# Queries of the first weight block split by token tile in the key-score stage of a two-block transformer kernel

## The chip, the cores and the metric

One core of a Trainium2 chip runs the whole program in one launch. The metric is the device time of that core in microseconds (us), median of several runs. Engines are named as in the profile: PE (TensorE matmul), PEld (its weight load), DVE (VectorE), ACT (ScalarE), POOL (GpSimd), SP (the queue that loads weights).

## The reference

Two layers of a latent/context block with a product-key expert layer, then two layers of a hybrid mixer with memory attention; 256 tokens, width 1024, fp32. The part that matters here is how the expert layer picks its experts:

```
def block(xc):                       # 128 tokens
    q = (xc @ wq).reshape(C, 8, 2, 128)                # 16 "half heads" of 128
    s = einsum('chpd,hpnd->chpn', q, sub_keys)         # 128 scores for each half head
    s1, i1 = top_k(s[:, :, 0], 16);  s2, i2 = top_k(s[:, :, 1], 16)
    cand = s1[..., :, None] + s2[..., None, :]         # 256 sums for each head
    top, pos = top_k(cand, 16);  eidx = cidx[pos]
    g = softmax(top)
    a = gelu(einsum('chkd,cd->chk', u_tab[eidx], xc))
    return einsum('chk,chkd->cd', g * a, v_tab[eidx])
```

The modulation vectors of both layers (silu(c) @ ada_w, six times 1024 values for each layer) are also needed; the kernel spreads that product over other stages.

## The kernel before, in words

The program is a row of stages. Each is a block in which every engine has its own list of instructions, and a barrier closes it. A stage is written once and can run in three settings: alone; beside the modulation sums (`run_with_sums`, L437); or as a guest inside an expert stage, beside the gathers (`run_guest`). The test `hosted()` is true in the last setting only.

**The key-score stage** (`keys_stage`, L1799) runs for token pair s of layer l. The tokens are two tiles of 128. PE turns the 16 sub-key matrices (L1819) and DVE copies them to SBUF (L1854). Then comes a list of items. An item is one half head h for one tile or for both. PE computes the query of the item: 8 matmuls of 128 x 128 weights with 256 columns (both tiles) or 128 (one tile), L1830; the trace shows two records for each. ACT copies it (L1891), PE multiplies it with the keys (`dot`, L1847; one matmul a tile), and ACT copies the scores to `sims` (L1896). PE issues the dot of item i after the product of item i+1, and the product of item i needs ACT's copy of item i-3. The weights of wq come in four blocks of four half heads. Before the change only block 3 is split by tile: 12 whole items, then 4 for tile 0 and 4 for tile 1, 20 in all (0 to 19).

**The search** runs on DVE in the same stage, for tile 0 of the pair only. For every quarter q (two heads, half heads 4q to 4q+3) there are three pieces: the top 16 of half heads 4q and 4q+1 (L1931 to L1935), the same of 4q+2 and 4q+3, then the candidates (L1953) and their top 16, followed by `pair_indices` (L1991 to L2014) for the quarters 0 to 2, and after quarter 0 the writing of the first picks (L2018, L2022). The first piece needs the scores of half head 4q+1, the others those of 4q+3. In the program's order a piece stands behind the step of item i as soon as the item that it needs is i-2 or lower. What is left of the picks of quarter 3 is done in the next stage, `last_picks` (L2024).

**The modulation sums** (`ModulationSums`) are a list of rows, 8 to a block, each 512 columns wide. For a block that both streams need, DVE makes one stream's step of a row (L846 for the first row of a block, L849 for the others), after which ACT scales the row for the other (L866), and POOL adds it (L884; the first row of a block needs no add). For a block of one stream only ACT and POOL work. The weights of four rows come in one DMA of 1 MB that POOL issues (L897) into one of two slots, when POOL has added the rows that were in the slot; at row 4n of its list it asks for the load of rows 4n+4 to 4n+7. When a block is added, PE sums it over the partitions (L911).

Where the rows stand among the other work is fixed by a pace when the program is written. Each item of the key stage is worth 5.0 us (both tiles), 2.15 us (tile 0) or 0 us (tile 1); DVE gets one row for every 2.0 us in layer 0 (`sums.host(keys, 2.0, ...)`, L2524) and for every 3.4 us in layer 1 (L2554), in both cases before the search pieces of that item. ACT does the rows that belong to item i before it copies the query of item i. Rows that are left go to `last_picks`: there ACT and POOL do them first. Layer 0 has rows up to 112, of which DVE has work in those below 96; the stage begins at row 77. Layer 1 has 48, the stage begins at row 32, and DVE has no work in any.

**What POOL does behind the rows**: in the key stage it issues the first 4 (layer 0) or 6 (layer 1) expert gathers; in `last_picks` it issues gathers up to row 6 (9), waits for all sums and issues three more. `last_picks` ends on DVE with an addition of the summed modulation (L966 in layer 0, L972 in layer 1), which waits for PE's last L911. The expert stage then starts with DVE's L2205 and its 512 gathered rows (L2226 and others).

The key stage runs outside an expert stage twice (layer 0 and layer 1, token pair 0), and once as a guest. In layer 1 it also ends with turned memory tiles: PE transposes four pairs into the PSUM banks 0 to 3 (`turn_memory`, L1809) and ACT takes them out with `gain_memory_pair`.

Of the kernel before, what the change touches and what calls it, by code (L numbers as in the profile page):

```python
# [127 lines left out]
def build_kernel(nc, io, out):  # L128
# [61 lines left out]
    def open_stage():  # L190
        for s in every:
            s.base = s.total
# [200 lines left out]
    def hosted():  # L393

        return host[0] and host[0].block
# [255 lines left out]
    def column(name, j):  # L651
        return columns[:, where[name][0] + j:where[name][0] + j + 1]
# [1146 lines left out]
    def keys_stage(l, s):  # L1799


        open_stage()
        split = (3,)
        items = [(4 * b + j, t, n) for b in range(4) for t, n in (((0, 1), (1, 1)) if b in split else ((0, 2),)) for j in range(4)]
        last = len(items) - 1
        keys_t = lifted[:, 2048 * s:2048 * s + 2048]
        qt = [proj[:, 2 * P * i:2 * P * (i + 1)] for i in range(4)]

        def turn_memory(pe):  # L1809
            for g in range(4):  # L1810
                if g == 3:
                    pe.wait_ge(*read_a.at(dots_at(last - 1)))
                turn_memory_pair(pe, g, g)

        def tensor(pe):
            w = take(pe, ("keys", l))
            for g in range(4):
                for q in range(4):
                    mm = pe.transpose(psum[:, g, q * P:q * P + P], w[:, 4 * g + q, :], ident)  # L1819
                mm.then_inc(*products.one())  # L1820
            release()
            for i, (h, t0, nt) in enumerate(items):
                if h % 4 == 0 and t0 == 0:
                    w = take(pe, ("wq", l, h // 4))
                yield 4 + asked_at(i)
                pe.wait_ge(*(emptied if hosted() else read_v).at(4))
                if i >= 3:
                    pe.wait_ge(*read_a.at(asked_at(i - 3)))
                for k in range(KD):
                    mm = pe.matmul(psum[:, i % 3, 0:P * nt], w[:, k, (h % 4) * P:(h % 4) * P + P],  # L1830
                                   turned_s[s][:, k, P * t0:P * (t0 + nt)], start=k == 0, stop=k == KD - 1)
                mm.then_inc(*products.one())
                if h % 4 == 3 and t0 + nt == 2:
                    release()
                if i >= 1:
                    dot(pe, i - 1)
            dot(pe, last)
            if l == 1:
                turn_memory(pe)
# [33 lines left out]
        def asked_at(i):  # L1873
            return 2 * i if i else 1

        def dots_at(i):
            return 2 * i + 3 if i < last else 2 * last + 2

        def scalar(act):
            for g in range(4 if hosted() else 0):  # L1880
                yield g + 1
                act.wait_ge(*products.at(g + 1))
                act.copy(keys_t[:, 512 * g:512 * g + 512], psum[:, g, :]).then_inc(*emptied.one())
            for i in range(last + 2):
                if i <= last:
                    w = P * items[i][2]
                    yield 4 + asked_at(i)
                    act.wait_ge(*products.at(4 + asked_at(i)))
                    if i >= 4:
                        act.wait_ge(*products.at(4 + dots_at(i - 4)))  # L1890
                    act.copy(qt[i % 4][:, 0:w], psum[:, i % 3, 0:w]).then_inc(*read_a.one())  # L1891
                if i >= 1:
                    h, t0, nt = items[i - 1]
                    yield 4 + dots_at(i - 1)
                    act.wait_ge(*products.at(4 + dots_at(i - 1)))
                    act.copy(sims[:, t0:t0 + nt, h, :], psum[:, 3 + (i - 1) % 3, 0:P * nt].rearrange("p (t n) -> p t n", t=nt))\  # L1896
                       .then_inc(*read_a.one())
            if l == 1:
                for g in range(4):
                    gain_memory_pair(act, 0, g, g)  # L1900

        run_stage(tensor, vector, scalar)
        if l == 0:
            lifted_free[s] = products.now()
# [590 lines left out]
    def to_keys(l, s):  # L2495

        tiles = [2 * s, 2 * s + 1]
        return [lambda: turn_mixed(s, HALVED),
                lambda: linear_stage([([("w_out", l, b)], "rows", tiles, normed, ("add", lambda t: gate_row(0, s), 512 * b))
                                      for b in range(2)], ahead=memory_root() if l == 1 else None),  # L2500
                lambda: norm_stage(tiles, lambda k, t: first_gain(1, k, s), lambda k, t: first_shift(1, k, s)),
                lambda: turn_back(s), lambda: keys_stage(l, s)]
# [115 lines left out]
    def turn_memory_pair(pe, g, bank):  # L2618
        for i in range(2):
            k = 2 * g + i  # L2620
            for t in range(2):
                mm = pe.transpose(psum[:, bank, 256 * i + P * t:256 * i + P * t + P], mixed_v[:, 2 + t, k * P:k * P + P], ident)
        mm.then_inc(*filled.one())

    def gain_memory_pair(act, l, g, bank):
        act.wait_ge(*filled.at(g + 1))
        for i in range(2):
            k = 2 * g + i
            ins = act.activation(turned_s[1][:, k, :], psum[:, bank, 256 * i:256 * i + 256], ACT.Copy,
                                 scale=column("norm_mem_w_2", 8 * l + k))  # L2630
        ins.then_inc(*emptied.one())
# [586 lines left out]
```

## Time and profile before

| | us |
| --- | --- |
| median of 3 runs | 3812.22 |
| runs | 3797.35 to 3813.24 |
| profiled execution, its own time | 3829.47 |
| its span | 3827.7 |
| PE busy | 2777.0 (73%) |
| DVE busy | 2517.3 (66%) |
| POOL busy | 1683.3 (44%) |
| ACT busy | 793.1 (21%) |
| layer 0, key stage and the picks after it | 363 to 453 |
| layer 1, the same | 2246 to 2326 |

A busy share is a mean over stages with different limits. What the change is worth is read from the two stretches of the last lines, 170 us of the span.

### The profile page before, as it was taken

The numbers are of one execution on the slowest core, as the hardware profiler recorded it, in microseconds if no ns is written. First come the engines' busy times: TensorE is split into PE (matmuls) and PEld (weight loads), VectorE is DVE, ScalarE is ACT, GpSimd is POOL, SyncE is SP. The second block draws the span as 40 slices with busy tenths as digits, with TensorE's granted clock in tenths as the row PEclk, the third lists the DMA queues.
The fourth block names the chain that finished last, engine by engine and source line by source line (L and its number), as shares of the span: only waits on it lengthen the run. The fifth ranks groups of instructions, "written<-read, shape, count | busy, mean of one in ns | idle before, by whom it ended". The sixth has DMA issues, their size and how long they took to land. (4 is left out here: it accounts for less than half of the span.)

```text
span 3827.7 us, 31086 instructions
## 1 busy us (share of the span) xinstructions
PE 2777.0 (73%) x8573; PEld 1444.4 (38%) x8573; DVE 2517.3 (66%) x5611; ACT 793.1 (21%) x2031; POOL 1683.3 (44%) x1722
## 2 busy tenths in 40 slices
PE   7998675777787676863086886358516799899998
PEld 3455632213462232221022565133202265566555
DVE  3665978777786678878855457887786536533542
ACT  2243200222122200210022431012002213410331
POOL 2333565674546555665665244667666600000000
PEclk9998888996899888986599897679758999999999
DMA  7534699998999899998999448999999954234321
GB/s 268 181 126 165 242 384 393 347 362 288 365 353 362 320 400 404 366 357 303 373 356 334 156 177 312 374 380 389 385 404 362 360 206 149 77 144 143 128 88 72
DMA packets 353335, 1086.55 MB, mean 284 GB/s; under 512 B 32657, under 2 KB 41357, under 8 KB 352013
## 3 DMA queue, kind: packets, MB, share of 16 engines
q0 software_dynamic: 232592, 849.45, 58.8%
q1 hardware_dynamic: 120572, 235.12, 17.4%
q8 instruction: 72, 1.18, 0.1%
q14 instruction: 99, 0.80, 0.1%
HBM read 1080.21 MB, written 4.24 MB: 283 GB/s over the span
## 5 line engine op out<-in xcount | busy, mean ns | idle before, releaser
L2260 ACT ACTIVATE heads<-common,dots 128x128 f32<-128x128 f32 x768 | 279.9, 396 | 778.0 <-PE psum L2276 362.4
L1269 PE MATMUL psum<-ring,turned 128*128 128x512 f32 (+1 forms) x800 | 344.4, 589 | 49.9 <-issue 32.1
L2226 DVE SCALAR_TENSOR_TENSOR lent<-lent,psum 128x1024 f32<-128x1024 f32 x274 | 323.2, 1218 | 48.6 <-ACTq L482 24.6
L2276 PE MATMUL psum<-lent,heads 128*128 128x512 f32 x524 | 289.0, 652 | 73.2 <-DMA lent<-in_peer_v_dram,picks_u 36.3
L2276 PE MATMUL psum<-proj,heads 128*128 128x512 f32 x374 | 207.3, 655 | 178.2 <-issue 160.2
L2316 POOL DMA_INDIRECT lent<-in_peer_u_dram,picks_u x274 | 257.4, 939 | 176.9 <-DVE lent L2226 90.3
L2316 POOL DMA_INDIRECT lent<-in_peer_v_dram,picks_u x262 | 251.4, 960 | 129.8 <-issue 61.0
L1721 PE MATMUL psum<-ring,turned 128*128 128x512 f32 x512 | 234.7, 617 | 38.4 <-issue 14.7
L2234 DVE SCALAR_TENSOR_TENSOR psum<-lent,dots,psum 128x512 f32<-128x512 f32 x262 | 197.8, 755 | 96.9 <-DMA lent<-in_peer_v_dram,picks_u 60.2
L2226 DVE SCALAR_TENSOR_TENSOR proj<-proj,psum 128x1024 f32<-128x1024 f32 x195 | 232.2, 1218 | 28.0 <-issue 14.4
L1269 PEld LDWEIGHTS psum<-ring,turned 128*128 128x128 f32 x800 | 161.0, 203 | 228.7 <-issue 216.9
L2276 PE MATMUL psum<-turned,heads 128*128 128x512 f32 x258 | 149.3, 681 | 132.2 <-issue 110.6
L2316 POOL DMA_INDIRECT proj<-in_peer_u_dram,picks_u x195 | 183.6, 941 | 117.4 <-DVE proj L2226 60.6
L2316 POOL DMA_INDIRECT proj<-in_peer_v_dram,picks_u x187 | 179.2, 958 | 101.5 <-issue 46.8
L2276 PEld LDWEIGHTS psum<-lent,heads 128*128 128x128 f32 x524 | 87.2, 195 | 271.1 <-DMA lent<-in_peer_v_dram,picks_u 181.3
L2234 DVE SCALAR_TENSOR_TENSOR psum<-proj,dots,psum 128x512 f32<-128x512 f32 x186 | 140.4, 755 | 70.1 <-DMA proj<-in_peer_v_dram,picks_u 43.0
L884 POOL TENSOR_TENSOR gate_rows<-heads,gate_rows 128x512 f32<-128x512 f32 x80 | 107.5, 1344 | 177.9 <-ACT heads L866 162.4
L2276 PEld LDWEIGHTS psum<-proj,heads 128*128 128x128 f32 x374 | 65.3, 199 | 310.9 <-issue 226.1
L2316 POOL DMA_INDIRECT turned<-in_peer_u_dram,picks_u x135 | 127.2, 942 | 125.3 <-DVE turned L2226 50.7
L2276 PE MATMUL psum<-heads 128*128 128x512 f32 x130 | 75.1, 661 | 137.8 <-ACT heads L2260 96.0
L2226 DVE SCALAR_TENSOR_TENSOR turned<-turned,psum 128x1024 f32<-128x1024 f32 x135 | 161.2, 1218 | 18.0 <-issue 8.7
L1721 PEld LDWEIGHTS psum<-ring,turned 128*128 128x128 f32 x512 | 100.2, 198 | 169.3 <-issue 141.8
(388 smaller groups left out, 5430.6 us busy)
## 6 DMA issues: line engine op xcount, KB each, us to landing
ring<-in_w_in_dram SPq DMA_DIRECT2D x37, 2048.0 KB
proj<-in_ada_w_dram POOLq DMA_DIRECT2D x20, 1024.0 KB, 5.7
heads<-in_ada_w_dram POOLq DMA_DIRECT2D x20, 1024.0 KB, 6.0
ring<-in_peer_wq_dram SPq DMA_DIRECT2D x10, 2048.0 KB
lent<-in_w_in_dram SPq DMA_DIRECT2D x9, 2048.0 KB, 7.8
ring<-in_w_out_dram SPq DMA_DIRECT2D x9, 2048.0 KB
lent<-in_w_out_dram SPq DMA_DIRECT2D x5, 2048.0 KB, 8.1
ring<-in_w_mk_dram SPq DMA_DIRECT2D x4, 2048.0 KB
```

What stands on the lines that cost most here:

```text
L884: pool.tensor_tensor(out=acc, in0=self.weights(self.row_pool), in1=acc, op=ALU.add)\
L1269: mm = pe.matmul(psum[:, b % nb, 0:cols], lhs(k, it), w[:, kk, :], start=k == 0, stop=k == k_total - 1)
L1721: mm = pe.matmul(psum[:, 2 * ((q + i) % deep), :], turned_s[place][:, k, i * P:i * P + P], w[:, k, :], start=k == 0, stop=k == KD - 1)
L2226: dve.scalar_tensor_tensor(out=src, in0=src, scalar=1.0, in1=kept_row, op0=ALU.mult, op1=ALU.mult, accum_out=weight).then_inc(rows_used.se ...
L2234: dve.scalar_tensor_tensor(out=acc, in0=part, scalar=weight, in1=acc, op0=ALU.mult, op1=ALU.add)\
L2260: act.activation(diags[n % DIAGS], ident, ACT.Copy, scale=dots[:, j:j + 1]).then_inc(diag_ready.sem, 1)
L2276: pe.matmul(kept_row[:, 0:512], diags[n % DIAGS], row_slot(r)[:, 0:512], start=j == 0, stop=j == PICKS - 1).then_inc(pe_rows.sem, 1)
L2316: pool.indirect_dma_start(out=row_slot(r), out_offset=None, in_=tables_dram[which], in_offset=bass.IndirectOffsetOnAxis(ap=picks_u[:, t, j ...
```

## The change

Where the stage is not a guest of an expert stage, block 0 of wq is split like block 3. The items are then 24 (0 to 23): the four half heads of block 0 for tile 0, the same four for tile 1, 4 whole items each for blocks 1 and 2, and block 3 as before. Item 0 to 3 are worth 2.15 us each to the pace and items 4 to 7 nothing. Layer 1's fourth memory pair goes to the bank that the last dot but one has left, now bank 4 and no longer bank 3.

```diff
         open_stage()
-        split = (3,)
+        split = (3,) if hosted() else (0, 3)
         items = [(4 * b + j, t, n) for b in range(4) for t, n in (((0, 1), (1, 1)) if b in split else ((0, 2),)) for j in range(4)]
         last = len(items) - 1
+        free_bank = 3 + (last - 1) % 3
...
                 if g == 3:
                     pe.wait_ge(*read_a.at(dots_at(last - 1)))
-                turn_memory_pair(pe, g, g)
+                turn_memory_pair(pe, g, g if g < 3 else free_bank)
...
                 for g in range(4):
-                    gain_memory_pair(act, 0, g, g)
+                    gain_memory_pair(act, 0, g, g if g < 3 else free_bank)
```

## Rows read from the trace of the kernel before

**Rows 1.** Waits of the layer 0 stretch (363 to 453): total us, times, longest.

```profile
DVE gate_rows L849 <- DMA heads<-in_ada_w_dram: 6.9, 1, 6.9
```

**Rows 2.** Timeline, start of layer 0's stage: start, us, engine, line, [idle before].

```profile
363.15 3.39 DVE L849 SCALAR_TENSOR_TENSOR gate_rows<-heads,silu_c,gate_rows 128x512 f32<-128x512 f32 x3
367.99 2.33 DVE L849 SCALAR_TENSOR_TENSOR gate_rows<-proj,silu_c,gate_rows 128x512 f32<-128x512 f32 x3
368.75 0.37 ACT L1891 COPY proj<-psum 128x256 f32<-128x256 f32 x1 [3.31 <-PE psum L1830]
371.74 0.77 POOL L897 DMA_DIRECT2D heads<-in_ada_w_dram  x1 [0.30 <-POOL gate_rows L884]
377.23 2.33 DVE L849 SCALAR_TENSOR_TENSOR gate_rows<-heads,silu_c,gate_rows 128x512 f32<-128x512 f32 x3 [6.91 <-DMA heads<-in_ada_w_dram]
379.47 0.48 DVE L1931 MAX8 heads<-proj 128x8 f32<-128x128 f32 x2
387.24 0.48 DVE L1931 MAX8 heads<-proj 128x8 f32<-128x128 f32 x2
```

**Rows 3.** Timeline of PE, layer 0: whole and half products, a step apart.

```profile
413.54 3.62 PE L1830 MATMUL psum<-turned,ring 128*128 128x256 f32 x16
417.44 3.62 PE L1830 MATMUL psum<-turned,ring 128*128 128x256 f32 x16
426.47 1.95 PE L1830 MATMUL psum<-turned,ring 128*128 128x128 f32 x16
428.48 1.95 PE L1830 MATMUL psum<-turned,ring 128*128 128x128 f32 x16
```

**Rows 4.** Timeline of DVE, layer 0: quarters 1 and 2.

```profile
398.33 5.08 DVE L849 SCALAR_TENSOR_TENSOR gate_rows<-heads,silu_c,gate_rows 128x512 f32<-128x512 f32 x4
407.10 0.49 DVE L1931 MAX8 heads<-proj 128x8 f32<-128x128 f32 x2 [1.35 <-ACT proj L1896]
412.45 0.20 DVE L1991 CAST heads<-heads 128x64 f32<-128x64 uint32 x1
419.39 3.53 DVE L2011 TENSOR_TENSOR lifted<-lifted,heads 128x512 f32<-128x512 f32 x2
431.70 0.41 DVE L1991 CAST heads<-heads 128x64 f32<-128x64 uint32 x1
434.81 1.32 DVE L2011 TENSOR_TENSOR lifted<-lifted,heads 128x512 f32<-128x512 f32 x2
```

**Rows 5.** Timeline of POOL, PE and DVE, layer 0: adds, and the picks stage.

```profile
412.77 5.55 POOL L884 TENSOR_TENSOR gate_rows<-heads,gate_rows 128x512 f32<-128x512 f32 x4 [0.47 <-ACT heads L866]
445.46 0.20 DVE L1991 CAST heads<-heads 128x64 f32<-128x64 uint32 x1 [0.60 <-PEq L438]
446.24 1.29 POOL L884 TENSOR_TENSOR gate_rows<-heads,gate_rows 128x512 f32<-128x512 f32 x1 [9.88 <-ACTq L438]
447.68 1.84 PE L911 MATMUL psum<-common,gate_rows 128*128 128x1 f32 x8 [8.36 <-POOL gate_rows L884]
452.27 0.39 DVE L966 TENSOR_TENSOR soft<-psum,columns 128x32 f32<-128x32 f32 x2
453.03 0.93 POOL L2316 DMA_INDIRECT heads<-in_peer_u_dram,picks_u  x1 [0.30 <-POOLq L438]
453.23 1.23 DVE L2205 COPY psum<-mixed 128x1024 f32<-128x1024 f32 x1 [0.57 <-PEq L438]
```

**Rows 6.** Timeline, layer 1's stage.

```profile
2248.74 7.15 PE L1830 MATMUL psum<-turned,lent 128*128 128x256 f32 x32 [1.36 <-DVE lifted L1854]
2260.67 0.49 DVE L1931 MAX8 heads<-proj 128x8 f32<-128x128 f32 x2 [12.08 <-ACT proj L1896]
2268.47 0.49 DVE L1931 MAX8 heads<-proj 128x8 f32<-128x128 f32 x2 [5.36 <-ACT proj L1896]
2283.67 0.37 ACT L1896 COPY proj<-psum 128x256 f32<-128x256 f32 x1
2285.81 0.46 DVE L1931 MAX8 heads<-proj 128x8 f32<-128x128 f32 x2
```

## The prediction

> **What bounds the kernel now.** PE and DVE are the busiest engines over the span, but the change touches only two stretches of it, so I read the waits of those stretches first and then their timelines engine by engine. The reader is to see that the search on DVE sets the end of both key stages, and what makes it late.
>
> In layer 0 it is not the scores. DVE idles 6.9 us for the weights of a sum row [rows 1] and only 1.35 us for scores [rows 4]. Ten rows stand ahead of the first search piece (items 0 to 3, 20 us at one row for 2.0 us). DVE is through seven by 370.3, waits until 377.23 for the load that POOL issued at 371.74 (5.5 us), and searches from 379.47 [rows 2]. After that it has no wait but the 1.35 us at 407.10 [rows 4].
>
> In layer 1 DVE has no row work and does wait for scores: 12.08 us, then 5.36 us; from 2268.47 on it has work to the end of the stage [rows 6].
>
> **PE's share.** A whole item takes 3.90 us from start to start (413.54 to 417.44), a half one 2.01 us (426.47 to 428.48), both with their dots [rows 3]. Block 0 costs 8 x 2.01 = 16.1 instead of 4 x 3.90 = 15.6 us: 0.5 us more for every later item; between nothing and 1 us. Four more copies of each kind on ACT hide between products: ACT waited 3.31 us for the first one [rows 2].
>
> **Order in layer 0, changed.** The pace now gives 4 rows (77 to 80) for items 0 to 3, none for 4 to 7, then 2, 3, 2, 3, 2, 3 for items 8 to 13, 2 and 3 for 14 and 15, and one each for 16 to 19: the stage ends at 77 + 57.2/2 = row 105. Before it was 77 + 68.6/2 = 111. So six rows, 105 to 110, move behind the stage.
>
> *Quarter 0.* DVE is through row 80 at 368.0. Item 0 is delayed by the slow clock at the start: its copy came at 368.75 where 3.6 us of product from 363.4 give 367.0, so 1.7 us. Half items then end near 367.0 and 368.8, the dot of item 1 after item 2 at 371.0, its copy at 371.6: the search starts there, 7.9 us sooner. The first piece took 2.3 us, so 374.0; item 3's scores are copied at 375.6 (two items later), and the rest of quarter 0 with the first picks takes 398.33 - 387.24 = 11.1 us [rows 2, 4]: 386.7, where before it was 398.3. So far 11.6 us are gained, but before DVE had rows 77 to 91 done there, and now has 77 to 80.
>
> *The rows that are late.* Rows 81 to 83 take 0.78 us each beside a quiet POOL [rows 2], to 389.0; 84 to 87 at 1.13 to 393.5. POOL has added row 83 at 392.6 (ACT's scaling, then 1.39 us a row [rows 5]), so only now asks for rows 88 to 91: 392.9 + 5.5 = 398.4. DVE stands idle 4.9 us. Before, that load was hidden behind the search. Rows 88 to 90 to 401.8; the first piece of quarter 1 from there, against 403.4 (398.33 + 5.08) [rows 4]; then rows 91 to 95, five of 1.1 us, which before were done: 401.8 + 2.4 + 5.6 = 409.8, where the second piece began at 407.10. **The stage is 2.7 us later** from there on. Quarters 1 to 3 have the same work. Bounds: 0 (if the five rows find POOL quiet and the load lands in 3 us) to 6 (if the load of rows 92 to 95 is waited for as well).
>
> *A contended port.* In quarter 1, L2011's two instructions took 3.53 us with POOL adding beside them; in quarter 2, 1.32 us [rows 4]. From its first instruction to the end of L2011 the index work took 412.45 to 422.92 in quarter 1, 10.5 us, and 431.70 to 436.13 in quarter 2, 4.4 us: 6 us of blocking. In the changed order POOL's adds for rows 97 to 103 fall at about 415 to 427, on quarter 1's index work again, so I add nothing here; 0 to 3 us either way. The Trainium skill (SBUF — State Buffer, on port contention) says that DVE and GpSimd share a port pair, that one instruction holds it to its end and the other blocks. By that rule six adds moved beside the last index work would stretch it too; this trace agrees with 3.53 against 1.32 us.
>
> *Picks stage.* Before, one add (row 111) was left to it: POOL 446.24 to 447.53, PE's L911 to 449.5, and DVE's index work hid both, reaching L966 at 452.27, 6.8 us after its start [rows 5]. Now seven adds are left (105 to 111): 0.8 + 7 x 1.42 = 10.7 us after the start, PE 2.0, DVE's wake-up 0.1, so L966 at 12.8. **That is 6.0 us more.** The index work, 6.8 us before and stretched by up to those 6 us, stays just under it. POOL's gathers of rows 4 to 8 begin 8.7 us later relative to the stage; before, the last began 0.2 us ahead of the barrier, and the first four gathers are in already; DVE uses row 4 some 6 us after the barrier, so I take no stall. If the barrier waits for their issue it is 1.5 to 3 us more. Bounds 5 to 9 us.
>
> Layer 0: 2.7 + 6.0 = 8.7 us later.
>
> **Layer 1.** Rows need no DVE, so the search starts with the scores. From 2248.74: item 1 to 2252.3, item 2 with dot 0, dot 1, copy: 2255.1 instead of 2260.67. The second piece at 2259.1 instead of 2268.47, that is 9.4 us sooner [rows 6]; quarter 0 ends at 2274.1 instead of 2283.5. But item 9 (half head 5) has its scores only at 2276.7, and item 11 (half head 7) 0.5 us after their old 2284.0 (copy of 2283.67 + 0.37): 2284.5. Before, DVE came for them at 2285.81 [rows 6], only 1.8 us behind. **Of 9.4 us, 1.3 are left.** Then the adds: before, all 16 rows were issued by item 10 and POOL turned to gathers before quarter 1; now they run to item 18, beside the index work of quarters 1 and 2. What quarter 0 loses to adds lies inside the slack that DVE now has; three adds beside quarter 1 cost up to 2 us, of which I take 0.8. All 48 rows are done in the stage (57.2/3.4 = 16.8), so the picks stage keeps its size. I take -1.3 + 0.8 = -0.5 us, bounds -3 to +4.
>
> The bank change orders nothing new: the same last dot but one is waited for. It is nothing, or half a microsecond for the later PE end, under the search by 1.8 us.
>
> **Sum.** +8.7 - 0.5 = +8.2 us. The profiled execution, 3829.5, would be 3837.7. It stands 17.3 us (0.45%) over the median of the runs shown; with the same difference on 3812.2 I forecast 3820.4.
>
> **Rivals.**
>
> 1. *The head start is kept* (faster). For: DVE has 8.3 us of idle in layer 0 and 17.4 in layer 1 ahead of the search. If the load of rows 88 to 91 came in time and POOL took its seven adds under the index work, layer 0 would win 8.3 - 3.6 - 1.6 = 3; in layer 1 up to 9.4 if quarter 1 did not catch up with PE. Some 12 us: 3800. Against: PE has no gap in which to bring item 11 forward. Chance 0.17.
> 2. *The late sums cost more* (slower than the forecast, and clearly slower than before). One mechanism: rows displaced behind the search make POOL late. It decides from the point at which the barrier after the picks holds until POOL has issued its five gathers: start + 10.9 + 5 x 1.25 + 0.5 = 17.7 instead of 7.8, so +9.9 and not +6; with 2.7, and 4 in layer 1 from adds beside two index runs, 17 us: 3829. For: gathers are issued by the same engine in order. Against: the last one started only 0.2 us before DVE's next work. Chance 0.18.
> 3. *Nothing is seen*: later work makes up what the start loses, because the expert stage waits on gathers, not on DVE's start; 3812. Against: POOL itself starts its gathers 11 us later in layer 0. Chance 0.15.
>
> The forecast itself: 0.50; its own range 3813 to 3828.
>
> **From these to the numbers.** About 0.5% (19 us) is what a measurement of this kernel can tell from no change. Every case above is inside it except part of rival 2 (17 us with an uncertainty of some 6) and what the 16 us between the runs shown add on either side. Faster 0.11, same 0.73, slower 0.16. The range 3798 to 3837 takes in rivals 1 to 3.
>
> **What would show it.** In layer 0: first L1931 near 371.6; L846 and L849 of rows 88 to 90 only after quarter 0, with an idle on a DMA of ada_w of about 5 us ahead of them; seven L884 after the last block line and L966 waiting for PE; L2205 near 462. In layer 1: first L1931 near 2255 relative to the old 2260.7, a wait of 2 to 3 us ahead of quarter 1 and one of 5 ahead of its second piece, the stage's end within 2 us of its old length. Wrong would be: no DMA wait in layer 0 (then it is nearer rival 1), L966 not waiting for PE's L911, or quarter 1 of layer 1 starting its second piece more than 3 us sooner.

## The result, and the profile after

The changed kernel takes 3825.36 us (median of 8 runs), the kernel before 3809.29 us (8 runs). The ratio is 1.0038, 95% interval 1.0023 to 1.0054: 14.5 us slower (8.8 to 20.6), inside the 0.5% that the prediction called "same", yet the interval leaves out zero. The two medians lie 16.1 us apart. The forecast was +8.2 us.

One profiled execution of each can't show this: the changed kernel's (3824.36 us) is 5.1 us shorter than that of before, since the work outside the two stretches differs from run to run by more than the change is worth: from the end of the first stretch to the start of the second it took 1792.9 us before, 1772.4 us after, and 1789.5 us in e1, whose layer 0 code is the same as that of the changed kernel. What repeats is the length of the two stretches. From here on **the layer 0 stretch** runs from DVE's first sum row in the key stage to the start of the expert stage (L2205, now L2206), and **the layer 1 stretch** from the first key copy to the same point. Layer 0: 453.23 - 363.15 = 90.08 us before, 472.09 - 368.13 = 103.96 after. Layer 1: 79.52 and 78.95. Together +13.3 us.

The timeline of DVE in layer 0, changed kernel (start, us, engine, line, [idle before it]), answers to [rows 2, 4]:

```profile
368.13 3.39 DVE L849 SCALAR_TENSOR_TENSOR gate_rows<-heads,silu_c,gate_rows 128x512 f32<-128x512 f32 x3
...
376.48 0.49 DVE L1932 MAX8 heads<-proj 128x8 f32<-128x128 f32 x2 [4.56 <-ACT proj L1897]
...
380.50 0.49 DVE L1932 MAX8 heads<-proj 128x8 f32<-128x128 f32 x2 [1.58 <-ACT proj L1897]
...
391.61 3.41 DVE L849 SCALAR_TENSOR_TENSOR gate_rows<-proj,silu_c,gate_rows 128x512 f32<-128x512 f32 x3
395.12 7.30 DVE L849 SCALAR_TENSOR_TENSOR gate_rows<-heads,silu_c,gate_rows 128x512 f32<-128x512 f32 x4
403.73 1.51 DVE L846 TENSOR_SCALAR gate_rows<-proj,silu_c 128x512 f32<-128x512 f32 x1 [1.30 <-DMA proj<-in_ada_w_dram]
...
406.74 0.48 DVE L1932 MAX8 heads<-proj 128x8 f32<-128x128 f32 x2
...
415.40 5.09 DVE L849 SCALAR_TENSOR_TENSOR gate_rows<-heads,silu_c,gate_rows 128x512 f32<-128x512 f32 x4 [5.31 <-DMA heads<-in_ada_w_dram]
420.40 0.48 DVE L1932 MAX8 heads<-proj 128x8 f32<-128x128 f32 x2
...
431.76 3.43 DVE L2012 TENSOR_TENSOR lifted<-lifted,heads 128x512 f32<-128x512 f32 x2
...
446.89 1.29 DVE L2012 TENSOR_TENSOR lifted<-lifted,heads 128x512 f32<-128x512 f32 x2
```

Take 368.13 off and compare with 363.15 taken off before: the search starts at +8.35 instead of +16.32, quarter 0 ends at +23.5 instead of +35.2, and then the gain is gone. The second piece of quarter 1 starts at +52.3 instead of +44.0, although its first piece is 1.6 us sooner (+38.6 instead of +40.2). Rows 91 to 95 now stand between the two pieces, and four of them waited 5.31 us for weights that before lay there.

POOL, PE and DVE at the end of the stretch, changed kernel, answering to [rows 5]:

```profile
457.52 0.19 DVE L1992 CAST heads<-heads 128x64 f32<-128x64 uint32 x1 [0.60 <-PEq L438]
458.30 4.13 POOL L884 TENSOR_TENSOR gate_rows<-proj,gate_rows 128x512 f32<-128x512 f32 x3 [15.81 <-ACT proj L866]
462.57 6.53 POOL L884 TENSOR_TENSOR gate_rows<-heads,gate_rows 128x512 f32<-128x512 f32 x4
464.56 3.41 DVE L2012 TENSOR_TENSOR lifted<-lifted,heads 128x512 f32<-128x512 f32 x2
469.25 1.84 PE L911 MATMUL psum<-common,gate_rows 128*128 128x1 f32 x8 [9.74 <-POOL gate_rows L884]
471.12 0.39 DVE L966 TENSOR_TENSOR soft<-psum,columns 128x32 f32<-128x32 f32 x2 [1.42 <-PE psum L911]
472.09 1.23 DVE L2206 COPY psum<-mixed 128x1024 f32<-128x1024 f32 x1 [0.57 <-PEq L438]
474.31 0.94 POOL L2317 DMA_INDIRECT heads<-in_peer_u_dram,picks_u  x1 [0.30 <-issue]
```

Seven adds stand where one stood, L966 waits for them, and the stage takes 14.6 us instead of 7.8. The last line shows that the barrier does not wait for POOL's gathers: the fifth starts 2.2 us after DVE has begun the expert stage. (The kernel opens these blocks with `no_gpsimd_drain=True`; no run does without it.)

Layer 1, DVE, changed kernel, answering to [rows 6]:

```profile
2253.48 0.49 DVE L1932 MAX8 heads<-proj 128x8 f32<-128x128 f32 x2 [6.52 <-ACT proj L1897]
2257.51 0.49 DVE L1932 MAX8 heads<-proj 128x8 f32<-128x128 f32 x2 [1.58 <-ACT proj L1897]
2275.12 0.49 DVE L1932 MAX8 heads<-proj 128x8 f32<-128x128 f32 x2 [4.19 <-ACT proj L1897]
2282.92 0.49 DVE L1932 MAX8 heads<-proj 128x8 f32<-128x128 f32 x2 [5.36 <-ACT proj L1897]
...
2323.43 1.23 DVE L2206 COPY psum<-mixed 128x1024 f32<-128x1024 f32 x1 [0.58 <-PEq L438]
```

DVE starts 5.6 us sooner relative to the stage. It then stands 4.19 us ahead of quarter 1's first piece and 5.36 us ahead of its second, 9.6 us where before it waited for no scores.

### The profile page after: what moved, and what is told of

It reads as the page before. It is cut to its first block and busy times, and to the rows that moved or that the text cites. A ratio compares the mean times of both kernels' runs of the same rounds, so it can differ in the third digit from the quotient of the medians.

```text
span 3822.6 us, 31382 instructions
## 1 busy us (share of the span) xinstructions
PE 2789.8 (73%) x8701; PEld 1455.1 (38%) x8701; DVE 2524.9 (66%) x5611; ACT 793.3 (21%) x2047; POOL 1683.6 (44%) x1722
## 5 line engine op out<-in xcount | busy, mean ns | idle before, releaser
L1269 PE MATMUL psum<-ring,turned 128*128 128x512 f32 (+1 forms) x800 | 335.3, 577 | 46.2 <-issue 31.9
L1721 PE MATMUL psum<-ring,turned 128*128 128x512 f32 x512 | 240.7, 630 | 37.1 <-issue 17.6
L1269 PEld LDWEIGHTS psum<-ring,turned 128*128 128x128 f32 x800 | 156.8, 198 | 220.4 <-issue 211.9
L884 POOL TENSOR_TENSOR gate_rows<-proj,gate_rows 128x512 f32<-128x512 f32 x60 | 79.6, 1327 | 211.2 <-ACT proj L866 207.3
```

The costliest lines, as they stand in the source:

```text
L884: pool.tensor_tensor(out=acc, in0=self.weights(self.row_pool), in1=acc, op=ALU.add)\
L1269: mm = pe.matmul(psum[:, b % nb, 0:cols], lhs(k, it), w[:, kk, :], start=k == 0, stop=k == k_total - 1)
L1721: mm = pe.matmul(psum[:, 2 * ((q + i) % deep), :], turned_s[place][:, k, i * P:i * P + P], w[:, k, :], start=k == 0, stop=k == KD - 1)
```

## The experiments

The stretches are read from one profiled execution each. "Index work" is the time at which the first index instruction of a quarter starts, from the start of the stretch; the fourth is the start of the picks stage. Ratios are to the kernel before, timed together with the run; "profiled once" stands where a run has no such timing.

| run | first piece | index work 0, 1, 2 | picks stage | layer 0 | layer 1 | ratio (95%) |
| --- | --- | --- | --- | --- | --- | --- |
| before | 16.3 | 29.4, 49.3, 68.6 | 82.3 | 90.1 | 79.5 | 1 |
| changed | 8.4 | 17.7, 57.6, 75.8 | 89.4 | 104.0 | 79.0 | 1.0038 (1.0023 to 1.0054) |
| e1 layer 0 only | 8.2 | 17.6, 57.4, 75.7 | 89.2 | 103.8 | 79.4 | 1.0034 (1.0017 to 1.0052) |
| e2 layer 1 only | 14.6 | 27.8, 47.7, 66.7 | 80.5 | 88.3 | 79.0 | 1.0009 (0.9988 to 1.0030) |
| e3 pace of before for items 0 to 3 | 15.1 | 22.8, 59.0, 78.0 | 94.2 | 101.9 | 78.2 | 1.0027 (1.0011 to 1.0043) |
| e4 pace 1.6 | 6.6 | 16.0, 54.6, 73.6 | 91.2 | 98.1 | 79.0 | profiled once |
| e5 DVE order of before | 15.9 | 29.5, 59.2, 77.4 | 91.0 | 98.8 | 79.0 | 1.0018 (1.0004 to 1.0033) |
| e6 2 MB load left out | 8.2 | 17.6, 53.9, 72.1 | 85.7 | 100.2 | 79.0 | profiled once |
| e7 rows fed by item | 9.1 | 17.8, 49.3, 68.3 | 86.0 | 92.8 | 79.0 | 0.9999 (0.9983 to 1.0015) |
| e8 rows fed by item, no split | 13.8 | 29.4, 51.8, 70.2 | 87.0 | 93.8 | 79.4 | profiled once |
| e9 narrow adds | 6.6 | 16.0, 45.2, 60.7 | 74.4 | 82.1 | 79.0 | profiled once |
| e10 e5, ACT and PE later | 17.4 | 31.1, 50.4, 70.1 | 86.7 | 94.5 | 79.0 | 1.0022 (1.0009 to 1.0035) |
| e11 e7, later; more split | 8.0 | 16.0, 54.8, 70.9 | 89.7 | 96.6 | 78.7 | 1.0020 (1.0006 to 1.0033) |

The same layer 0 code gave 90.1 and 88.3 us (before, e2), and 104.0 and 103.8 (changed, e1), so I read nothing into 2 us. Most of that is the granted clock of PE in the first products of the stretch, which was 0.50 (1.2 GHz) from 368 to 371 us in the changed kernel and 1.00 (2.4 GHz) in e4:

```profile
368.37 5.55 PE L1831 MATMUL psum<-turned,lent 128*128 128x128 f32 x32 [0.88 <-DVE lifted L1855]
```

```profile
367.65 3.81 PE L1831 MATMUL psum<-turned,lent 128*128 128x128 f32 x32 [1.36 <-DVE lifted L1855]
```

The first is the changed kernel, the second e4: 1.7 us between them for the same two half products, and the first search piece comes 1.7 us sooner in e4 (+6.6). Two whole products took 8.79 us before and 7.14 in e2. e2, e3, e4, e7, e9 and e11 had the short first products; before, changed, e1, e5, e6, e8 and e10 the long ones. Up to 1.7 us of a difference between the two groups is that and not the edit.

Runs e9 to e11 were timed together with a kernel before of 3677.19 us (mean granted clock 0.88), e5 to e8 with one of 3809.23 us (e5 and e7 at 0.87 and 0.86). Why the later runs are faster throughout is not known. Their ratios compare with the others, their times do not; the layer 1 stretch of e9 and e10 is 79.0 us as in the earlier runs.

**e1 and e2: which layer.**

```diff
-split = (3,) if hosted() else (0, 3)
+split = (3,) if hosted() or l == 1 else (0, 3)     # e1
+split = (3,) if hosted() or l == 0 else (0, 3)     # e2
```

> The split in layer 0 only. The layer 0 stretch runs from DVE's first sum row in the key stage to the first instruction of the expert stage (before 90.1 us, changed kernel 104.0 us); the layer 1 stretch from the first key copy to the same point (before 79.5, changed 79.0). Theory (the whole loss is in layer 0): stretches 104 and 79.5, ratio to before near 1.0035. Rival (the loss comes from both places, or from code that only differs in placement): ratio below 1.002.

> The split in layer 1 only. Theory (scores 9 us sooner, but PE holds quarter 1): stretches 90.1 in layer 0 and 79.0 in layer 1, ratio 0.999 to 1.001. Rival (head start kept in layer 1, hidden by other differences): layer 1 stretch near 72, ratio 0.998 or lower.

Both came as the theory said, but for e2's layer 0 stretch, 88.3 us for 90.1, of which 1.7 is the clock named above. The loss is in layer 0 (ratio 1.0034 alone); layer 1 alone is indistinguishable from before, with its stretch 0.6 us shorter.

**e4: what the late adds cost in the picks stage.**

```diff
-        sums.host(keys, 2.0, then_rows=...)
+        sums.host(keys, 1.6, then_rows=...)
```

> The full change with one row for 1.6 us instead of 2.0 in layer 0's key stage: 57.2/1.6 = 35.75, so all 35 rows are done in the stage and none is left for the picks stage. Theory (6.8 us of the loss is POOL's seven adds in the picks stage): from the first index instruction of the picks stage to L966 it takes 6.8 us or less (changed kernel 13.6), with the two L2004 and L2012 instructions at 1.3 us each instead of 3.4. The key stage before it stays at 88 to 92 us (changed 89.4 to its barrier; before 82.3). Rival (PE's sum or the barrier sets it): over 10 us.

The picks stage takes 6.9 us instead of 14.6 (5.9 us to L966, the index pairs at 1.29 and 1.32 us), so 7.7 us hung on the seven adds. Not all of it is won: quarter 2 now has the adds beside it and takes 91.2 - 73.6 = 17.6 us instead of 13.6. The stretch falls by 5.9 us, of which up to 1.7 is the clock of the first products.

**e6: why the load was slow.** In the kernel before, SP issued wq's block 3 at 399.17 and POOL its next load of 1 MB at 406.25; DVE or ACT had such loads after 5.5 to 5.7 us. In the changed kernel the two met, and the load took 415.40 - 405.26 = 10.1 us. First the queues of the changed kernel (SP, then POOL), then DVE in e6:

```profile
403.64 0.37 SPq L370 DMA_DIRECT2D ring<-in_peer_wq_dram  x1
```

```profile
405.26 0.77 POOL L897 DMA_DIRECT2D heads<-in_ada_w_dram  x1 [0.30 <-POOL gate_rows L884]
```

```profile
406.67 5.58 DVE L852 SCALAR_TENSOR_TENSOR gate_rows<-heads,silu_c,gate_rows 128x512 f32<-128x512 f32 x4 [1.41 <-DMA heads<-in_ada_w_dram]
```

```diff
             plan_block(("wq", l, b), io["peer_wq"][l], 512 * b, 512 * b + 512)
+            if b == 3 and l == 0:      # 16 columns of 512: queries of block 3 from what the slot held
+                key, cols, parts = plan[-1]
+                plan[-1] = (key, cols, [(0, P, parts[0][2][:, 0:8, 0:16])])
```

> The full change; in layer 0 the load of wq's block 3 brings 8 x 16 columns instead of 8 x 512 (2 MB less; the queries of block 3 are then made from what the slot held). Theory (the load of rows 92 to 95 took 10.1 us because it was issued 1.3 us after that 2 MB load): it lands in 5.5 to 6 us, DVE's wait ahead of rows 92 to 95 falls from 5.3 to about 1 us and the layer 0 stretch from 104.0 to 99 to 100. Rival (the load is slow by itself, or the wait only moves to the next one): stretch stays within 1 us of 104.

In e6 POOL issued the load at 400.94 and DVE had it at 406.67: 5.7 us. The wait fell from 5.31 to 1.41 and the stretch by 3.7 us, to 100.2, just above the 99 to 100 expected. So the meeting of the two loads cost about 4 us. (The load was issued 1.6 us after the other, not 1.3 as written there.) The DMA engines' share in the changed kernel says the same: 0.95 at 354 GB/s in the 6 us in which they overlap, against 0.58 at 171 GB/s in e6. The Trainium skill (DMA: Bandwidth & Descriptors, Queues, rings and completion order) says that a DMA engine alternates between the queue rows that have work, packet by packet. By that rule, as an estimate of mine, a 1 MB load beside a 2 MB one takes near twice as long; the 10.1 against 5.7 us agree.

**e9: the shared port.**

```diff
-                    pool.tensor_tensor(out=acc, in0=self.weights(self.row_pool), in1=acc, op=ALU.add)
+                    if self.count == 112 and self.row_pool > 80:      # 16 of 512 columns are added
+                        acc, w = acc[:, 0:16], w[:, 0:16]
+                    pool.tensor_tensor(out=acc, in0=w, in1=acc, op=ALU.add)
```

> The full change; POOL adds 16 of the 512 columns of every sum row from 81 on (the rest of those modulation sums is left out), everything else as it is. Theory (POOL's adds block DVE's index work through a port that they share, and the seven late adds hold up the picks stage): from the first index instruction of quarter 1 to that of quarter 2 13.6 us (changed kernel 18.2), the picks stage 8 us (14.6), L2004 and L2012 at 1.3 us each pair in every quarter; rows 84 to 87 on DVE about 3.5 us instead of 7.3; layer 0 stretch 84 to 90. Rival (the index work is slow for its own waits, not POOL's adds): quarter 1 stays at 18 us and only the picks stage gets shorter.

DVE in e9, rows 84 to 87, the scores it waits for in quarter 2, and the index work of quarter 1 and of the picks stage:

```profile
390.71 3.11 DVE L849 SCALAR_TENSOR_TENSOR gate_rows<-heads,silu_c,gate_rows 128x512 f32<-128x512 f32 x4
...
414.68 1.33 DVE L2014 TENSOR_TENSOR lifted<-lifted,heads 128x512 f32<-128x512 f32 x2
421.86 0.49 DVE L1934 MAX8 heads<-proj 128x8 f32<-128x128 f32 x2 [2.32 <-ACT proj L1899]
...
443.91 1.33 DVE L2014 TENSOR_TENSOR lifted<-lifted,heads 128x512 f32<-128x512 f32 x2
```

L2012's pair (here L2014) takes 1.33 us in both places, against 3.43 and 3.41 in the changed kernel, and four rows take 3.11 us against 7.30. Quarter 1 takes 15.5 us with a wait of 2.3 us for scores in it, so 13.2 us without, against 18.2. The stretch falls to 82.1, 8 us under before and below the range expected (84 to 90). So the blocking that the prediction put down to a contended port is real, and POOL's wide adds cause it: DVE paid for them in the rows, in quarter 1 and in the picks stage. That a port is the means no run here separates from other ways in which the two engines could collide. By the table, of the 22 us that e9 is shorter than the changed kernel, 1.7 lie ahead of the first index work (the clock of the first products), 10.7 between there and quarter 1's index work, 2.7 in quarter 1 and 6.8 in the picks stage. They are not all blocking: POOL's chain of adds and loads is faster too, and the load of rows 92 to 95, issued at 395.36, is no longer waited for.

**e3, e5 and e10: is it the place of the rows?** (Code shortened; `worth` holds in layer 0 only, where the pace is then 1.0.)

```diff
-yield (5.0 if items[i][2] == 2 else 2.15 ...), 4 + asked_at(i)
+yield (5.0 if items[i][2] == 2 or (i < 4 and not hosted()) else 2.15 ...), 4 + asked_at(i)   # e3
+yield worth[i] ...      # e5, pace 1.0: rows item by item
+worth = [2, 3, 2, 3, 2, 3, 0, 0, 2, 1, 1, 1, 2, 3, 2, 3, 1, 1, 1, 1, 0, 0, 0, 0]
```

> The full change, but items 0 to 3 are worth 5.0 us to the pace again, so that the sum rows stand at the same search pieces as before and the stage ends at row 111. Theory (it is the displaced rows): layer 0 stretch back to 90 to 91 us with the 6.9 us wait for weights back ahead of the search, layer 1 as in the changed kernel within 1 us, ratio 0.999 to 1.001. Rival (the half products and their extra copies cost the time): layer 0 stretch stays above 100.

e3 missed by 11 us, and its 101.9 lies in the rival's range. That does not show the rival: e3 put ten rows back ahead of the first piece, but the five that belonged to items 4 and 5 stayed behind quarter 0, and nine of DVE's rows (87 to 95) then stood ahead of quarter 1. So e5 gave DVE exactly the order of before:

> The full change, with the number of sum rows given item by item so that DVE's instructions stand in exactly the order of the kernel before (10 rows ahead of the first search piece, 5 ahead of the second, 5 and 5 around quarter 1's first piece, 34 in all, one add left to the picks stage). Theory (where the rows stand among the search pieces, not the half products, costs the time; in the run before this one five rows had not come back to their places): layer 0 stretch 88 to 91 us (before 90.1, changed 104.0), picks stage 7.8. Rival (ACT does a row before it copies a query, so rows tied to later items hold up PE's scores, whatever DVE's order): stretch 95 or more, with waits on ACT's copy of the scores ahead of quarter 1.

The rival won: 98.8 us. PE shows where, in e5:

```profile
383.71 1.95 PE L1832 MATMUL psum<-turned,lent 128*128 128x128 f32 x16
387.90 0.49 PE L1849 MATMUL psum<-lifted,proj 128*128 128x128 f32 x2 [2.24 <-ACT proj L1893]
392.47 3.54 PE L911 MATMUL psum<-common,gate_rows 128*128 128x1 f32 x16 [4.08 <-POOL gate_rows L884]
395.88 3.38 PE L1832 MATMUL psum<-turned,lent 128*128 128x128 f32 x16
```

ACT does a row before it copies the query of its item, PE a block sum before its item's product. With 24 items the rows of the first search pieces hang on block 0's items for tile 1, which nobody waits for, and block 1 comes late: DVE then waits 4.08 and 5.36 us for scores.

```diff
-yield 4 + asked_at(i)                        # ACT, PE
+yield 4 + asked_at(max(i - late, 0))         # late: 2 for ACT (dots as well), 4 for PE
```

> The kernel with DVE's instructions in exactly the order of before (run e5), but in layer 0 ACT does the rows of an item two items later and PE the block sums four items later. Theory (in e5 PE stood from 387.9 to 395.9 because ACT and PE must do the rows tied to items 4 and 5 ahead of queries that nobody waits for yet): that gap goes, DVE's waits for scores ahead of quarter 1 (4.1 and 5.4 us) go to under 2 us together, layer 0 stretch from 98.8 to 88 to 92. Rival (PE is the bound in layer 0 too, with 0.5 us and two whole products between the scores that DVE needs): stretch 95 or more.

The gap went, and so did both waits for scores (0.84 us is left), but the stretch came to 94.5, in neither range. Quarters 1 and 2 take 19.7 and 16.6 us (before 19.3 and 13.8); I put the difference down to POOL's adds, begun later, which now ran beside both. Ratio 1.0022.

**e7, e8 and e11: can the head start be used?** (Code shortened as above.)

```diff
+worth = [2, 2, 2, 1, 0, 0, 0, 0, 0, 1, 3, 4, 2, 2, 3, 3, 2, 2, 2, 2, 2, 0, 0, 0]   # e7, e11
+worth = [2, 2, 2, 1, 2, 2, 2, 2, 2, 2, 3, 3, 2, 2, 2, 2, 2, 0, 0, 0]               # e8, split = (3,)
+split = (3,) if hosted() else (0, 1, 3) if l else (0, 3)                            # e11, and 2.4 in layer 1
```

> The full change, rows placed by item in layer 0 so that DVE has work while it waits for scores and each load is asked for in time: 7 rows ahead of the first piece, none in quarter 0, 8 ahead of quarter 1's first piece, 4 ahead of its second, then 16, none left to the picks stage. Theory: first piece at +8.4 us as in the changed kernel, no wait for weights ahead of quarter 1, layer 0 stretch 84 to 88 us (before 90.1). Rival (POOL's chain of adds and loads needs rows steadily and becomes the bound): stretch 92 or more.

> The kernel before, without the split, rows placed by item in layer 0: 7 ahead of the first search piece, 4 ahead of the second, 4 and 4 around quarter 1's first piece, all 35 in the stage. Theory (the wait of 6.9 us for weights was due to the place of the rows alone): first piece at +9.5 us instead of +16.3, second near +19.5 when item 3's scores are there, layer 0 stretch 86 to 88 us. So the split itself would be worth at most 1 to 2 us in layer 0. Rival (it is the split that gives the time): stretch 90 or more.

> The kernel of e7 (rows placed by item, none left to the picks stage) with the same delay of ACT and PE in layer 0, and in layer 1 wq's block 1 split too, with one row for 2.4 us. Theory for layer 0: the wait of 2.6 us for scores goes, stretch 88 to 91 (e7 92.8, before 90.1), since POOL's adds still run beside two quarters' index work. Theory for layer 1: DVE has its scores in time, but PE and ACT end the stage at +70 us from the first key copy, so the stretch is 77 to 78 us (before 79.5, changed 79.0). Ratio to before 0.998 to 1.000. Rival for layer 1 (PE's end does not bind): 72 or less.

All three missed in layer 0. e7 removed every wait for weights but 0.8 us and the picks stage is short (6.9), yet quarters 1 and 2 take 19.0 and 17.7 us, where a quiet one takes 13.6. It is 11.2 us shorter than the changed kernel and its ratio is 0.9999; it beats nothing. e8, a like feeding without the split, takes 93.8: 3.7 us more than before, and 1.0 more than e7, which is within what the clock of the first products can do. So such feeding gives nothing over the kernel before, with the split or without it. e8 missed for another reason first. Its wait for weights ahead of the search is gone, but DVE stood 6.67 us for scores in its place, and the search began at +13.8 and not at +9.5. The first line is DVE in e8, the second ACT in the kernel before, copying the scores of item 1:

```profile
381.88 0.49 DVE L1932 MAX8 heads<-proj 128x8 f32<-128x128 f32 x2 [6.67 <-ACT proj L1897]
```

```profile
378.34 0.37 ACT L1896 COPY proj<-psum 128x256 f32<-128x256 f32 x1
```

Before, those scores were ready at 378.71 and the search began at 379.47. The 6.9 us wait for weights hid a wait for scores that ended only 0.8 us earlier. In e8 the index work of quarter 0 starts at +29.4, as before, and the time is lost behind it, in quarters 1 and 2 and after them (22.4, 18.4 and 16.8 us, before 19.9, 19.3 and 13.8, from index work to index work).

e11 ran into a wait of 12.0 us for weights: ACT's rows came later, so POOL's request did. Its ratio, 1.0020, is outside the range as well. In layer 1 the range of 77 to 78 was missed by 0.7: DVE had its scores for quarter 1, then waited 2.0 and 3.7 us in quarter 2, whose block was not split. PE hands out scores one quarter at a time; splitting two blocks only moved the wait.

## Why the prediction was right, and where it was off

By its own steps, from the start of the layer 0 stretch (363.15 before, 368.13 after):

| step | forecast | measured |
| --- | --- | --- |
| first piece | +8.45 | +8.35 |
| second piece | +12.45 | +12.4 |
| quarter 0 ends | +23.6 | +23.5 |
| row 88 starts | +35.3 | +35.6 |
| first piece of quarter 1 | +38.7 | +38.6 |
| second piece | +46.7 | +52.3 |
| picks stage starts, against before | +2.7 | +7.1 |
| picks stage, longer by | 6.0 | 6.8 |
| layer 0 | +8.7 | +13.9 |
| layer 1: first, second piece | 2255.1, 2259.1 | 2255.1, 2259.1 (1.63 added) |
| layer 1 | -0.5 | -0.6 |

- The mechanism held in the steps that were named: head start of 7.9 us, rows late, load asked for late, seven adds left, PE's end holding quarter 1 of layer 1. That the first piece agrees to 0.1 us has some luck in it: the forecast took over 1.7 us of slow clock from the trace of before, and the profiled run of the changed kernel had them too, e4 not (+6.6).
- The total forecast, 3820.4 us, stands 5.0 under the 3825.36 measured, but the kernel before came out 2.9 lower in its eight runs than in the three that the forecast was added to. By difference the forecast is +8.2 against +14.5: right in direction, a little over half the size.
- **One term was mis-sized**, "the stage is 2.7 us later". The load of rows 92 to 95 was taken as landed in time; its being waited for stood only as the upper bound (6). It took 10.1 us for 5.5, and the stage came 7.1 us later. e6 shows 4 us of it to be the meeting with wq's block 3, which SP issued 1.6 us earlier. The forecast had placed each load of POOL, but not SP's beside them. e6 is the test of that: with the meeting gone the stage is 3.4 us later than before, near the 2.7 forecast.
- Rows 84 to 87 took 7.3 us and not 4.5, with POOL adding beside them (3.1 us in e9). It cost nothing there, since the wait for row 88 shrank from the forecast 4.9 us to 1.3.
- Quarter 1's index work was 1.0 us shorter than before, inside the 0 to 3 given. The picks stage grew by 0.8 us more than forecast, inside its bounds.
- Rival 2 named the right direction, and its size (17 us) is nearer to the 14.5 than the forecast is, but its mechanism is refuted: the barrier was passed before two of POOL's gathers had started. Rival 1 is refuted for this placing of rows; the placing of e7 recovers 11 of 14 us, and whether another would do better was not run. Rival 3 is refuted by e1: ratio 1.0034 with a stretch 13.7 us longer, so the expert stage gives nothing back that could be measured.
- My reading of layer 0 as a question of where rows stand for DVE was too simple. e3 and e5 show the same place table holding up ACT and PE. And "in layer 0 it is not the scores" holds only for the wait that ended last: the scores of item 1 were ready 0.8 us before the search began, so with the weights in time and nothing else changed, that was all there was to win ahead of the search. (e8 begins 2.5 us sooner, since PE's block sum, too, moved behind the scores of item 1.)

Open: how much of e9's 22 us is blocking and how much the faster chain of POOL. The table says where they were gained, not by which of the two.

## What to carry to other kernels

When other work is paced by items, adding items shifts that work on every engine that follows the list, also on those that only copy or sum; count for each engine which item its next foreign row hangs on. Bringing one consumer's input forward is worth at most the slack with which its later inputs already arrive: in layer 1, 9.4 us turned into 0.6. The wait that a trace names is the one that ended last; look up when the other inputs were ready before counting it as a gain. For a load that moves, look up what every queue issues in that window, since a load's time is only its own when it is alone.

## What the runs showed of the hardware

- A 128 x 512 add on POOL (1.27 us) stretched a pair of 128 x 512 two-input instructions on DVE from 1.3 to 3.4 us, and some instructions of 0.18 us to between 1.1 and 1.3. With adds of 16 columns both went away (e9). Gathers issued by POOL beside the same work did not stretch the pair: L2011 took 1.32 us in quarter 2 of the kernel before [rows 4], with the third and fourth gather beside it:

```profile
433.66 1.44 POOL L2316 DMA_INDIRECT lent<-in_peer_u_dram,picks_u  x1 [0.30 <-issue]
435.40 0.95 POOL L2316 DMA_INDIRECT lent<-in_peer_u_dram,picks_u  x1 [0.30 <-issue]
```

- A 1 MB load took 5.5 to 5.7 us alone and 10.1 us when issued 1.6 us behind a 2 MB one.
- In these blocks, opened with `no_gpsimd_drain=True`, the barrier passed while gathers of POOL's list ahead of it were still to start: the last two of five began 1.0 and 2.2 us after DVE's first instruction of the next stage (changed kernel).
- A half product of 128 columns cost 2.01 us against 3.90 for 256, dots included: 3% more for the pair.
- The first two half products of layer 0's stage took 5.55 us where the granted clock was 0.50 (1.2 GHz) until 371 us and rose within them (changed kernel), and 3.81 us where it was 1.00 (2.4 GHz) throughout (e4, which differs only in the pace of the rows).
